# Layer norm behind the hybrid mixers: GpSimd adds the first five tiles, one weight half moves behind the last tile

## What is computed

```python
for l in range(DEPTH):                       # DEPTH = 2
    x = layer_norm(alpha * x + 0.5 * swiglu_2(x, w_ff1_in[l], w_ff1_out[l]), ln1_g[l], ln1_b[l])
    mix = hybrid_mixer(x, w_in[l], ...)
    x = layer_norm(alpha * x + mix, ln2_g[l], ln2_b[l])          # the norm t0, t1 of this text
    x = layer_norm(alpha * x + 0.5 * swiglu_2(x, w_ff2_in[l], w_ff2_out[l]), ln3_g[l], ln3_b[l])

def layer_norm(x, g, b):
    mu = mean(x); xc = x - mu; var = mean(xc * xc)
    return xc * rsqrt(var + 1e-5) * g + b
```

## Time and profile before

| | us |
|---|---|
| median of 3 runs | 2344.2 |
| lowest, highest | 2344.09, 2344.21 |
| the profiled execution | 2344.32 |
| its span | 2342.5 |
| outside the span | 1.8 |
| granted TensorE clock | 0.999 of full speed |

### The profile page before, as it was taken

How to read it: one execution, slowest core, us unless ns; L and a number is a source line. 1 busy time by engine, 2 the same in 40 slices (tenths; PEclk the granted TensorE clock), 3 DMA queues, 4 the chain that set the end, 5 groups by cost and what they waited for, 6 DMA issues and landing times.

```text
span 2342.5 us, 37935 instructions
## 1 busy us (share of the span) xinstructions
PE 2322.1 (99%) x15336; PEld 2120.1 (91%) x15336; DVE 1763.8 (75%) x2652; ACT 1276.7 (55%) x1993; POOL 79.8 (3%) x96
## 2 busy tenths in 40 slices
PE   8999999999999999999999999999999999999998
PEld 7988889998888888999999888998889999998887
DVE  6889657779758876887569886688767875698854
ACT  6855454655445544675555554455445855565542
POOL 0012000002100000020000000000000200000000
PEclk9999999999999999999999999999999999999999
DMA  6455565446556555654355555556555533456563
GB/s 227 136 185 193 188 207 166 145 158 210 177 183 208 189 187 186 200 163 125 118 172 181 189 189 182 169 194 202 188 189 190 175 119 120 160 171 223 188 184 107
DMA packets 115454, 412.48 MB, mean 176 GB/s; under 512 B 12880, under 2 KB 14800, under 8 KB 115024
## 3 DMA queue, kind: packets, MB, share of 16 engines
q1 hardware_dynamic: 114992, 407.96, 53.3%
q0 software_dynamic: 288, 2.10, 0.3%
HBM read 408.96 MB, written 1.05 MB: 175 GB/s over the span
## 4 chain that ended last, share of the span: by engine, by line
PE 90%; DVE 7%; ACT 1%; POOL 1%; issue 1%; DMA 0%; SPq 0%; DVEq 0%; POOLq 0%; ACTq 0%
PE ps L423 89%; DVE wlo L1891 2%; DVE region L2605 1%; ACT region L1375 0%; PE ps L698 0%; ACT whi L1175 0%; POOL region L2991 0%; POOL region L2992 0%; DMA raw<-in_ew_c 0%; DVE xx L2113 0%; DVE region L2160 0%; DVE RX L2077 0%; DVE x L2106 0%; DVE x L1943 0%; DVE region L2163 0%
## 5 line engine op out<-in xcount | busy, mean ns | idle before, releaser
L423 PE MATMUL ps<-xx,whi 128*128 128x256 f32 (+1 forms) x4920 | 1239.0, 341 | 2.0 <-DVE xx L1951 0.9
L1891 DVE TENSOR_TENSOR wlo<-raw,whi 128x1024 fp32r<-128x1024 f32 (+3 forms) x772 | 927.6, 1208 | 292.0 <-ACT whi L1175 290.8
L1175 ACT ACTIVATE whi<-raw 128x1024 fp32r<-128x1024 f32 (+3 forms) x772 | 801.7, 1044 | 581.2 <-PE ps L423 540.7
L423 PE MATMUL ps<-xx,wlo 128*128 128x256 f32 x3696 | 833.2, 280 | 0.0
L423 PEld LDWEIGHTS ps<-xx,wlo 128*128 128x128 f32 x3696 | 699.2, 189 | 109.5
L423 PEld LDWEIGHTS ps<-xx,whi 128*128 128x128 f32 x4920 | 764.7, 190 | 7.4 <-issue 3.4
L423 PE MATMUL ps<-H,whi 128*128 128x512 f32 (+1 forms) x2144 | 546.6, 343 | 1.3 <-DVE wlo L1891 1.3
L423 PE MATMUL ps<-H,wlo 128*128 128x256 f32 x1632 | 364.8, 279 | 0.0
L423 PEld LDWEIGHTS ps<-H,wlo 128*128 128x128 f32 x1632 | 308.5, 189 | 49.8
L423 PEld LDWEIGHTS ps<-H,whi 128*128 128x128 f32 x2144 | 333.2, 190 | 2.5 <-issue 2.0
L1886 DVE TENSOR_REDUCE t<-ps 128x256 f32<-128x512 f32 x308 | 211.6, 689 | 46.0 <-PE ps L423 39.4
(11 more groups left out here) (293 smaller groups left out, 1556.9 us busy)
## 6 DMA issues: line engine op xcount, KB each, us to landing
raw<-in_sg SPq DMA_DIRECT2D x128, 512.0 KB, 4.1
raw<-in_su SPq DMA_DIRECT2D x128, 512.0 KB, 4.2
raw<-in_sd SPq DMA_DIRECT2D x128, 512.0 KB, 4.3
raw<-in_mw_g SPq DMA_DIRECT2D x48, 512.0 KB, 3.5
raw<-in_fg SPq DMA_DIRECT2D x44, 512.0 KB, 3.3
raw<-in_fu SPq DMA_DIRECT2D x44, 512.0 KB, 3.2
raw<-in_fd SPq DMA_DIRECT2D x32, 512.0 KB, 3.6
raw<-in_mw_a SPq DMA_DIRECT2D x24, 512.0 KB, 4.2
```

The costliest lines, as they stand in the source:

```text
L423: return e.matmul(out, lhsT, rhs, start=start, stop=stop, skip_group_check=True)
L1175: e.activation(m.whi[:, c % NHL, 0:cw], m.raw[:, c % NRAW, 0:cw], ACT.Copy).then_inc(s["whi"].h, s["whi"].up(c))
L1891: e.tensor_tensor(m.wlo[:, c % NHL, 0:cw], m.raw[:, c % NRAW, 0:cw], m.whi[:, c % NHL, 0:cw].bitcast(F32), ALU.subtract).then_inc(s["wlo"] ...
```

## The change

In each of the two norms t, four of the six additions into `R` leave DVE. GpSimd makes them in a new function `early_sums`, behind its part of the mixer: tiles 0+1, 2, 3 and 4, each as soon as the tile is centred (`ycen` 1 and 2) or added (`xadd` 3 and 4). It counts them in a new signal `psum`. DVE's addition of tile 5 waits for `psum` 4 instead of its own previous addition. DVE keeps all six additions of squares, and tiles 5 and 6 of the sum. Apart from that, in DVE's `layer_norm` with `late`, the weight half that stood at k = 6 now stands behind the last tile (k = 8).

```diff
     def norm_tile(st, names, n, nz, add, gemm, bank, late=False):
         elif n == 7:
             if late:
                 for k in range(1, 7):
-                    total(st, k, nz)
+                    if k > 4:
+                        total(st, k, nz)
                     squares(st, k)
             raw_low(st, names, 7)
     def total(st, k, nz):
         w.wait_ge(s["ycen"] if k < nz else s["xadd"], st, k)
-        if k > 1:
+        if k == 5 and st[0] == "t":
+            w.wait_ge(s["psum"], st, 4)
+        elif k > 1:
             w.wait_ge(s["ysum"], st, k - 1)
...
-            if k in ((3, 6) if late else (3, 6, 8)):
+            if k in ((3, 8) if late else (3, 6, 8)):
                 produce(1)
@@ gpsimd_program
+    def early_sums(l):
+        st, t = f"t{l}", m.R[:, 0, :]
+        w.wait_ge(s["merge"], l, 0, 3, 1)
+        for k in range(1, 5):
+            if k < 3:
+                w.wait_ge(s["ycen"], st, k)
+            else:
+                w.wait_ge(s["xadd"], st, k)
+            if k > 1:
+                w.wait_ge(s["psum"], st, k - 1)
+            e.tensor_tensor(t, m.x[:, 0, :] if k == 1 else t, m.x[:, k, :], ALU.add).then_inc(
+                s["psum"].h, s["psum"].up(st, k))
+
     for l in range(2):
         hybrid(l)
+        early_sums(l)
```

More of the change, by code:

```diff
@@ L345 @@
     "ysum",
+    "psum",
     "sqsum",
```

## The result

The changed kernel takes **2347.2 us** (median of 21 runs, 2347.03 to 2347.35) against 2344.2 (21 runs, 2344.05 to 2344.53): 3.0 us more, ratio 1.0013, 95% interval 1.0007 to 1.0019. The forecast was 2345.2, the top of its range 2346.8. The sign was right, and as foreseen the difference is under 0.2%, but three times the loss came. The span of the profiled execution grew by 2.8 us, from 2342.5 to 2345.3, at the same granted clock of 0.999. The changed one was 0.18 ahead before it came to the first edited norm, t0, which accounts for spans that lie 2.8 apart and medians that lie 3.0 apart.

What follows compares the result with a forecast made beforehand. PE, 99% busy, bounds the kernel and waits for DVE at two places a norm. A loss of 0.89 less a gain of 0.38 is +0.51 a norm, +1.0 in all: 2344.2 to 2345.2 us, range 2342.3 to 2346.8.

Steps and rivals of the forecast that it cites:

- What bounds the kernel: Whole kernel: PE is busy 99% of the span, so DVE and GpSimd edits pay only where PE waits for DVE.
- both places of its waiting: PE in each norm t: waits of 0.47 us at the statistics and 0.74 at the last two normalised tiles.
- the slack: Ahead of the statistics: tile 6's `RX` half can be 0.78 us late before PE waits for it.
- The price of an addition to DVE: Each GpSimd addition beside DVE's two-operand instructions: delays DVE by 0.5 us, bounds 0 to 0.75; 0.4 to 0.6 given 50%.
- The argument by exclusion: DVE beside GpSimd's additions: an exclusion that holds GpSimd off should hold DVE too, 0.5 us an addition.
- the first two rivals: GpSimd's additions: DVE isn't held up (2342.5, 25%); GpSimd only gets in beside one-operand DVE instructions (2343.4, 12%).
- The wait for GpSimd at nothing: DVE's addition of tile 5: GpSimd's additions end 4 us ahead of need, so waiting for them costs nothing.
- The step of dependent additions: DVE's four additions of squares in a row: each starts 0.04 after the one ahead ends, 0.45 us a step.
- The new wait for the weight half: End of each norm: PE waits 0.26 plus 0.10 us for chunk 7's moved half, in place of 0.74.
- the four prices of an addition: DVE's delay per GpSimd addition: 0, 0.27, 0.5 or 0.75 us, giving 2342.5, 2343.4, 2345.2 or 2347.2.
- each addition holds DVE for the whole 0.75: Rival on GpSimd's additions: DVE 3.0 us late, +1.51 a norm, 2347.2; whole instruction or worse given 11%.
- D: DVE's lateness in a norm from GpSimd's four additions; beyond 1.5 us, or 0.37 an addition, the change loses.

## Why the prediction was right in sign and too small

- **What bounds the kernel** held for PE's work: both places of its waiting moved with DVE, less the slack, and between the norms nothing changed.
- **The price of an addition to DVE**, on which the sign hung, was taken as 0.5 between bounds of 0 and 0.75. It measured 0.48 to 0.55. DVE's lateness of 2.0 came as 2.01 (2.06 of stretching, less 0.05 of gaps), and PE's wait for tile 6's `RX` half of 1.22 + 0.10 as 1.22 + 0.10. The argument by exclusion was right, and the first two rivals fall: DVE is held up, and the additions sat beside centrings and `RX` halves, not beside one-operand instructions. Tile 7 was added at 1239.12 (forecast 1239.3, in an execution that entered 0.18 earlier).
- **The wait for GpSimd at nothing** held: DVE never waited for `psum`, and the last addition was done at 1235.13.
- **The step of dependent additions** failed. The two dependent instructions of the earlier trace rows start 1.00 - 0.48 = 0.52 apart, 0.04 behind one another's end. The prediction carried the 0.04 over to the shorter additions, which gave 0.45; the 0.52 itself would have come close. The four squares measure (2.00 - 0.42) / 3 = **0.53** a step, where the interleaved ones take 0.34. Three steps of 0.08 more make the sum 0.24 later, and PE wants it at 1242.24 and starts at 1242.52: 0.28 instead of 0.04. This is the step of the forecast that failed inside the norm: a chained addition was costed at 0.45 and takes 0.53. The restart behind it, 0.11, was left out of the forecast. Together 0.35 a norm, **0.7 of the missing time**.
- **The new wait for the weight half** came where it was foreseen, at 0.37 + 0.09 instead of 0.26 + 0.10. DVE starts the half 0.41 after the last lower half (forecast 0.40), but PE begins 0.14 after its end (1258.51 + 1.22 = 1259.73 to 1259.87), not the 0.05 that was carried over from the sum. **Some 0.2 of the missing time.**
- **The end of the program** was not in the prediction at all: **1.10**. It counted nothing outside the two norms and so put this term at nothing without a reason. The runs show an instruction fetch in the last output transfer instead, and that twelve added instructions take it out again; the cause in between, that fewer instructions move DVE's code in the blocks in which it is fetched, is inferred.
- **The sum**: forecast 1.0; 0.7 + 0.2 + 1.1 more make 3.0, as measured (t1 lost a little less than t0). The range failed by the last term: it had been built from the four prices of an addition alone, and the changed kernel with the fetch out of the way takes 2346.27, inside it. The rival "each addition holds DVE for the whole 0.75" gave 2347.2, the time that came, and was wrong all the same. Its D of 3.0 and its wait of 2.22 are in no row. A right total is no proof of a mechanism. What failed in this rival is its price, the profiled length of the addition, 0.74 to 0.78 us, where DVE loses 0.48 to 0.55. The rule of the Trainium skill that was cited beside it ("for the whole instruction", page "SBUF — State Buffer") is neither confirmed nor refuted by that, since no row shows when within its profiled length GpSimd takes the ports and gives them back.

## What to carry to other kernels

GpSimd, reading SBUF beside a DVE that is full of instructions with two SBUF operands, does not relieve it: an addition taken off DVE saved 0.34 us and cost 0.48 to 0.55 when GpSimd made it, so look instead for a gap in DVE's own row (here a wait for ACT behind a moved weight half) and put the early additions there. When neighbours that hid each other's latency are taken apart, cost the chain that is left by its own step (0.53 against 0.34). And when instructions are removed, compare the landing of the last output before a difference of a microsecond is put down to the change itself.

## What the runs showed of the hardware

- GpSimd and DVE exclude each other in both directions while DVE reads two SBUF operands and GpSimd reads SBUF. DVE's reductions from PSUM show nothing of it: beside GpSimd they take 0.68 us, and all 308 of the kernel before lie between 0.679 and 0.694. A GpSimd addition of 128x256 float32 costs DVE 0.48 to 0.55 us whether it falls into a run of centrings or behind a weight half; a GpSimd memset of the same tile at the same place costs DVE nothing that its rows show, and isn't held up itself (0.31 us inside a weight half).
- The last instruction fetch, one packet of 8 KB, can fall into the last transfer of the output. With 2644 instructions on DVE's page line it comes 1.8 us behind the end of DVE's last one and the output lands after 3.14 us; with 2648 or more it comes earlier, and the output lands after 2.02 to 2.05. Twelve useless instructions took 0.93 us off the time. Whose code is fetched is inferred.
- PE starts 0.14 to 0.15 us behind the end of a weight half (128x1024) that it waits for, in all twelve such waits in the norms of six kernels, and 0.05 to 0.06 behind the end of a sum or a lower half (128x256).
- A 128x256 float32 addition on DVE takes 0.34 us a step among independent neighbours and 0.53 when each waits for the one ahead; its profiled length is 0.42 in both cases.
